# A fused transformer layer on one core: the last four experts' down projection by experts and by quarters, and the output in six transfers

## The reference, cut to what matters

```python
def rms_norm(x, g):
    y = x * lax.rsqrt(jnp.mean(x * x, axis=-1, keepdims=True) + 1e-6)
    return y * g

# h: (256, 2048). One layer: attention and a gated MLP branch, then a mixture of 32 experts
h = h + merged @ w_out
xn2 = rms_norm(h, norm_ffn_g)
# top-1 of 4 groups, top-2 of 8 experts in it; for each of the 32 experts e (FF = 256):
hid = silu(xn2 @ w_e_gate[e]) * (xn2 @ w_e_up[e])          # (tokens, 256)
h = h + combine[:, e] * (hid @ w_e_down[e])                # (tokens, 2048)
return rms_norm(h, norm_final_g)
```

## Time and profile before

| | us |
|---|---|
| runs (3) | 1019.73, 1020.6, 1021.96; median 1020.6 |
| the profiled execution's own time | 1020.6 |
| its span, first to last instruction | 1018.9 |
| around the span | 1.7 |
| mean granted TensorE clock over the span | 0.975 |

### The profile page before, as it was taken

One profiled execution on the slowest core, in us unless ns is written; L12 is line 12 of the kernel. 1 busy time (PEld: TensorE's weight loads), 2 busy tenths in 40 slices (PEclk: granted clock), 3 DMA queues, 4 the chain that ended last, 5 costly groups with the idle time before them and its releaser, 6 DMA issues.

```text
span 1018.9 us, 12972 instructions
## 1 busy us (share of the span) xinstructions
PE 960.7 (94%) x5174; PEld 676.3 (66%) x5174; DVE 392.4 (39%) x535; ACT 331.8 (33%) x482; POOL 2.7 (0%) x13
## 2 busy tenths in 40 slices
PE   8999999999999999999999889999999796979984
PEld 7888788788888888888888555737373541726331
DVE  5746666575555455565443212020202020120204
ACT  5435554744343333443444121121111110211123
POOL 1000000000000000000000000000000000000000
PEclk9999999999999999999999999999999897999978
DMA  9755555559656556666878999999999999999995
GB/s 322 257 196 196 161 159 189 170 176 292 204 197 210 194 193 218 217 246 215 292 285 292 413 421 391 424 420 421 421 421 420 421 421 422 420 421 421 421 400 194
DMA packets 93233, 310.15 MB, mean 304 GB/s; under 512 B 11464, under 2 KB 12544, under 8 KB 71424
## 3 DMA queue, kind: packets, MB, share of 16 engines
q1 hardware_dynamic: 93184, 309.45, 80.1%
HBM read 307.33 MB, written 2.10 MB: 304 GB/s over the span
## 4 chain that ended last, share of the span: by engine, by line
PE 70%; SPq 12%; DMA 12%; ACT 2%; issue 1%; DVE 1%; DVEq 0%; ACTq 0%
PE bank L1381 15%; PE bank L1383 15%; PE bank L1382 15%; SPq L448 12%; DMA pair<-in_w_e_up 10%; PE bank L1689 5%; PE bank L1747 5%; PE bank L1794 2%; PE bank L1708 2%; DMA pair<-in_w_e_down 1%; PE bank L1671 1%; PE bank L1697 1%; PE bank L1451 1%; PE bank L1459 1%; PE bank L1388 1%
## 5 line engine op out<-in xcount | busy, mean ns | idle before, releaser
L893 DVE TENSOR_TENSOR wlo<-raw,whi 128x2048 fp32r<-128x2048 f32 x91 | 208.4, 2291 | 194.6 <-ACT whi L545 194.6
L545 ACT ACTIVATE whi<-raw 128x2048 fp32r<-128x2048 f32 x91 | 174.4, 1917 | 251.0 <-PE bank L1383 246.6
L1381 PE MATMUL bank<-whi,actT_hi 128*128 128x512 f32 x576 | 227.0, 394 | 0.6 <-DVE wlo L893 0.5
L1383 PE MATMUL bank<-wlo,actT_hi 128*128 128x512 f32 x576 | 224.4, 390 | 0.0
L1382 PE MATMUL bank<-whi,actT_lo 128*128 128x512 f32 x576 | 224.2, 389 | 0.0
L1689 PE MATMUL bank<-pair,xe 128*32 128x512 f32 x896 | 118.4, 663 | 22.7 <-DMA pair<-in_w_e_up 22.6
L1381 PEld LDWEIGHTS bank<-whi,actT_hi 128*128 128x128 f32 x576 | 108.2, 188 | 24.0 <-DVE wlo L893 1.2
L1383 PEld LDWEIGHTS bank<-wlo,actT_hi 128*128 128x128 f32 x576 | 108.1, 188 | 22.8
L1382 PEld LDWEIGHTS bank<-whi,actT_lo 128*128 128x128 f32 x576 | 108.2, 188 | 21.6
L1747 PEld LDWEIGHTS bank<-sel,resid 128*128 128x128 f32 x480 | 105.9, 311 | 9.0 <-issue 7.8
L1747 PE MATMUL bank<-sel,resid 128*128 128x128 f32 x480 | 108.6, 384 | 1.0 <-DVE sel L1226 1.0
(11 more groups left out here) (215 smaller groups left out, 724.8 us busy)
## 6 DMA issues: line engine op xcount, KB each, us to landing
pair<-in_w_e_down SPq DMA_DIRECT2D x64, 1024.0 KB, 26.1
pair<-in_w_e_gate SPq DMA_DIRECT2D x56, 1024.0 KB, 26.5
pair<-in_w_e_up SPq DMA_DIRECT2D x56, 1024.0 KB, 26.1
raw<-in_w_gate SPq DMA_DIRECT2D x64, 512.0 KB, 4.5
raw<-in_w_in SPq DMA_DIRECT2D x56, 512.0 KB, 4.8
raw<-in_w_out SPq DMA_DIRECT2D x32, 512.0 KB, 4.8
raw<-in_w_branch_a SPq DMA_DIRECT2D x16, 512.0 KB, 4.5
raw<-in_w_branch_b SPq DMA_DIRECT2D x16, 512.0 KB, 4.6
```

The lines of the kernel that those rows point to most:

```text
L545: return act.activation(whi[slot][:], src, ACT.Copy)
L893: dve.tensor_tensor(wlo[s][:], raw[:, k, :], whi[s][:], ALU.subtract).then_inc(lo_made, 1)
L1381: pe.matmul(o, x_hi, w_hi, start=start, stop=False)
L1383: return pe.matmul(o, x_hi, w_lo, start=False, stop=stop)
```

## The change

Only the last quad and what follows it.

- **Weights.** The first four down pieces of the last quad are those of the other quads: one expert, half f=0, all columns, 8 KB rows. The last four are one block, half f=1, all four experts, 2 KB rows.
- **TensorE.** It waits for all four f=0 pieces, then computes f=0 of blocks 0, 1, 2 and of the first 256 columns of block 3. Then for b = 0, 1, 2: f=1 of block b and at once the scatter of block b; behind that of block 0, f=0 of the second 256 columns of block 3, in bank 2, which is free by then. Then f=1 of both halves of block 3, and the scatter in four quarters of 256 columns, banks 6, 7, 0, 1.
- **Evictions of block 3.** ScalarE takes the first half, VectorE the second.
- **Squares.** Block 3 has four quarters: three on ScalarE, the last on VectorE by a `scalar_tensor_tensor` with an accumulator. `ssq_f` gets a fifth column.
- **The mean.** The step L904 goes: ScalarE takes the root with scale 1/D and a bias tile `eps`, which GpSimd fills at the start of the kernel, and VectorE takes the reciprocal behind it.
- **Output.** `times_gain` is made for blocks 0 and 1 alone. ScalarE multiplies these by the reciprocal root, block by block; VectorE computes blocks 2 and 3 from `resid`, root and gain in one instruction each. Six transfers: four of 256 KB for tile 0, two of 512 KB for tile 1.

The diff, without the branch for tokens over capacity:

```diff
         def down_at(qd, f, e):
-            return PIECES * qd + 4 * QUAD + (2 * e + f if qd == LAST else QUAD * f + e)
+            return PIECES * qd + 4 * QUAD + QUAD * f + e
...
-            return ((6, 7, 0, 1, 2, 3, 4, 5)[u] if qd == LAST else 6 + t), b, t
+            return ((6, 7, 0, 1, 3, 4)[u] if qd == LAST else 6 + t), b, t
+        def last_quarter(i):
+            h, t = divmod(i, TT)
+            return (6, 7, 0, 1)[i], slice(HALF * h, HALF * h + HALF), t
...
+            for h in range(2):
+                sp.wait_ge(y_by_act, h + 1)
+                leave(0, h * COLS, h * COLS + COLS)
+                sp.wait_ge(y_by_dve, h + 1)
+                leave(0, D // 2 + h * COLS, D // 2 + h * COLS + COLS)
+            sp.wait_ge(y_by_act, 4)
+            leave(1, 0, D // 2)
+            sp.wait_ge(y_by_dve, 4)
+            leave(1, D // 2, D)
...
             output_rows_out(LAST, 0)
-            for b in range(1, NC):
-                final_squares(b - 1, sq_f_made, range(0, 1))
-                output_rows_out(LAST, b)
-                final_squares(b - 1, sq_f_made, range(1, 2))
-            final_squares(NC - 1, sq_f_made)
+            for b in range(1, NC - 1):
+                output_rows_out(LAST, b)
+                for t in range(TT):
+                    final_squares(b - 1, t, sq_f_made)
+            final_squares(NC - 2, 0, sq_f_made)
+            act.wait_ge(d_full, NC * LAST + NC)
+            act.activation(out_rows[NC - 1][:, 0:HALF], bank[5][:, 0:HALF], ACT.Copy).then_inc(rows_made, 1)
+            final_squares(NC - 2, 1, sq_f_made)
+            for i in range(3):
+                last_squares(i, sq_f_made)
...
-            root(3)
+            act.wait_ge(ssq_made, 4 * TT)
+            act.activation(ms[:, 3 * TT:4 * TT], ssq[:, 3 * TT:4 * TT], ACT.Sqrt, scale=1.0 / D,
+                           bias=eps[:, 0:1]).then_inc(ms_made, TT)
+            act.wait_ge(rstd_made, 4 * TT)
+            act.wait_ge(hf_early, TT * 2)
             for t in range(TT):
                 n = 3 * TT + t
-                act.activation(y_out[:, t, ACT_COLS], y_out[:, t, ACT_COLS], ACT.Copy,
-                               scale=rstd[:, n:n + 1]).then_inc(y_by_act, 1)
+                for b in range(2):
+                    cols = slice(b * COLS, (b + 1) * COLS)
+                    act.activation(y_out[:, t, cols], y_out[:, t, cols], ACT.Copy,
+                                   scale=rstd[:, n:n + 1]).then_inc(y_by_act, 1)
...
+            dve.wait_ge(d_full, NC * LAST + NC + 1)
+            dve.tensor_copy(out_rows[NC - 1][:, HALF:COLS], bank[2][:, HALF:COLS]).then_inc(rows_late, 1)
+            for i in range(4):
+                dst, cols, t = last_quarter(i)
+                dve.wait_ge(scat_full, 8 * LAST + TT * (NC - 1) + i + 1)
+                h = resid[:, t, (NC - 1) * COLS + cols.start:(NC - 1) * COLS + cols.stop]
+                dve.tensor_tensor(h, bank[dst][:, cols], h, ALU.add).then_inc(added, 1)
+            dve.wait_ge(added, 8 * NQ + 2)
+            order.link(dve.scalar_tensor_tensor(out=sq2[:, 1, D - HALF:D], in0=resid[:, 1, D - HALF:D], scalar=1.0,
+                                                in1=resid[:, 1, D - HALF:D], op0=ALU.mult, op1=ALU.mult,
+                                                accum_out=ssq_f[:, 1, NC:NC + 1]))
...
             dve.tensor_reduce(ssq[:, 3 * TT:4 * TT], ssq_f[:], AX_X, ALU.add).then_inc(ssq_made, TT)
-            inverse_mean(3, D)
...
+            dve.wait_ge(ms_made, 4 * TT)
+            dve.reciprocal(rstd[:, 3 * TT:4 * TT], ms[:, 3 * TT:4 * TT]).then_inc(rstd_made, TT)
...
+                for b in range(2, NC):
+                    cols = slice(b * COLS, (b + 1) * COLS)
+                    dve.scalar_tensor_tensor(out=y_out[:, t, cols], in0=resid[:, t, cols], scalar=rstd[:, n:n + 1],
+                                             in1=gfin[:, cols], op0=ALU.mult, op1=ALU.mult).then_inc(y_by_dve, 1)
...
+            for e in range(QUAD):
+                n = down_at(LAST, 0, e)
+                pe.wait_ge(slot_in[n % RING], arrived(n))
             for b in range(NC):
-                for f in range(2):
-                    n = down_at(LAST, f, b)
-                    pe.wait_ge(slot_in[n % RING], arrived(n))
-                    if f == 0:
-                        pe.wait_ge(rows_made, NC * (LAST - 1) + b + 1)
-                    down_block(LAST, f, b)
-                    if f == 0 and b:
-                        scatter(LAST, range(TT * b - TT, TT * b))
-            scatter(LAST, range(TT * NC - TT, TT * NC))
+                pe.wait_ge(rows_made, NC * (LAST - 1) + b + 1)
+                last_down(0, 2 + b, b, whole if b < NC - 1 else first_half)
+            for b in range(NC - 1):
+                n = down_at(LAST, 1, b)
+                pe.wait_ge(slot_in[n % RING], arrived(n))
+                last_down(1, 2 + b, b, whole)
+                scatter(LAST, range(TT * b, TT * b + TT))
+                if b == 0:
+                    last_down(0, 2, NC - 1, second_half)
+            n = down_at(LAST, 1, NC - 1)
+            pe.wait_ge(slot_in[n % RING], arrived(n))
+            last_down(1, 5, NC - 1, first_half)
+            last_down(1, 2, NC - 1, second_half)
+            for i in range(4):
+                dst, cols, t = last_quarter(i)
+                pe.wait_ge(added, 8 * LAST + i + 1)
...
+                pe.matmul(bank[dst][:, cols], selT[:, t * P:(t + 1) * P], out_rows[NC - 1][:, cols],
+                          start=True, stop=True).then_inc(scat_full, 1)
```

More of the change, by code:

```diff
@@ L190, in build_trunk @@
         table_junk = small("table_junk", [P, 1])
+        eps = small("eps", [P, 1])
         bsT = small("bsT", [P, SG])
@@ L528, in _ @@
             pool.memset(wspT[:], 0.0).then_inc(pool_order, 1)
-            order.n = 6
+            pool.memset(eps[:], EPS).then_inc(pool_order, 1)
+            order.n = 7
             order.wait()
@@ new lines, in _ @@
+            whole, first_half, second_half = slice(0, COLS), slice(0, HALF), slice(HALF, COLS)
+            for e in range(QUAD):
+                n = down_at(LAST, 0, e)
+                pe.wait_ge(slot_in[n % RING], arrived(n))
+            for b in range(NC):
+                pe.wait_ge(rows_made, NC * (LAST - 1) + b + 1)
+                last_down(0, 2 + b, b, whole if b < NC - 1 else first_half)
+            for b in range(NC - 1):
+                n = down_at(LAST, 1, b)
[4 more added lines that the diff above has]
+                    last_down(0, 2, NC - 1, second_half)
@@ new lines, in _ @@
+            n = down_at(LAST, 1, NC - 1)
+            pe.wait_ge(slot_in[n % RING], arrived(n))
+            last_down(1, 5, NC - 1, first_half)
+            last_down(1, 2, NC - 1, second_half)
+            for i in range(4):
+                dst, cols, t = last_quarter(i)
+                pe.wait_ge(added, 8 * LAST + i + 1)
+                if i < TT:
+                    pe.wait_ge(rows_made, NC * LAST + NC)
+                else:
+                    pe.wait_ge(rows_late, 1)
+                pe.matmul(bank[dst][:, cols], selT[:, t * P:(t + 1) * P], out_rows[NC - 1][:, cols],
+                          start=True, stop=True).then_inc(scat_full, 1)
```

92 lines of the change are left out of this document (46 added, 46 removed).

## The result

| | us |
|---|---|
| changed kernel, median of 7 runs | 1024.88 (1023.45 to 1027.99) |
| kernel before, beside it | 1020.21 (1019.61 to 1021.96) |
| ratio | 1.0046, 95% interval 1.0035 to 1.0056 |
| profiled execution | 1027.99, span 1026.2 |

The change costs 4.7 us, in the direction of the forecast and nearly twice its size.

The account below looks back on a forecast made before the run. The prediction took the weights' stream as the bound before and TensorE after the change. Last add 2.86 us later, less 0.40 us in the tail, gave +2.5 on 1020.6: 1023.1, stated as 1023.0, range 1021.8 to 1024.2 (8 in 10: 1020.4 to 1024.7).

Parts of the forecast that it names:

- What bounds: At the end, the weights' stream decides today when the last block starts; after the change TensorE ends last, by 4.6 us.
- The weights' stream: Last quad's down pieces: 8 KB rows save 0.87 us, last landing about 1003.66; f=0 waits for the fourth piece at 991.85.
- rival (c): Last quad's weights: rows of 8 KB bring nothing, fourth piece lands at 992.7, total 1023.9 us; chance 0.10.
- The clock: TensorE in f=0, behind 4.65 us idle: one 3.4 us stretch at half clock, costing 1.7 us.
- Rival (b): TensorE: f=0 and the first f=1 both at half clock, 1.7 us more, total 1024.7 us; chance 0.10.
- Block 3 in halves: Last block, f=1 start to end of last add: 3.66 us instead of 4.52, 0.86 us gained.
- The mean: From last add to first output issue: 2.32 us, 0.53 us sooner than before.
- The output: From first output issue to end of span: 6.95 us plus about 0.13 for 2 KB rows.
- step of 3.7 us: Start of block 3's f=1 on TensorE moves from 1004.57 to 1008.3, 3.7 us later.
- (a): TensorE's clock stays up through f=0, 1.7 us less, total 1021.4 us; chance 0.15.
- (d): Start of the last block: the stream still decides it, gain 2.1 us, total 1018.5 us; chance 0.08.
- (e): Last quad and tail: scatter order doesn't matter, loss in front is won back in the tail, 1020.6 us; chance 0.07.

Follow-up runs that it names:

- after again: The changed kernel run and profiled once more with no edit: 1024.63 us, ratio 1.0028.
- `front_only`: Kernel before with only the new f=0 pieces, wait for all four and order of down blocks; old tail: 1025.17 us, ratio 1.0032.
- `tail_only`: Changed kernel with the down pieces and block order of before, keeping the split last block, new mean and six transfers: 1019.70 us, ratio 0.9980.
- `clock_kept_3`: Changed kernel plus three matmuls of unused result while TensorE waits for the fourth f=0 piece: 1023.51 us, ratio 1.0032.
- `hole_filled`: Changed kernel with each scatter behind the next block's f=1, and ScalarE's block 3 eviction ahead of block 2's squares: 1022.42 us, ratio 1.0022.
- `tail_branch`: `tail_only` with VectorE's square moved behind the branch for tokens over capacity: 1019.75 us, ratio 0.9989; again 1019.91 us, ratio 0.9992.
- `before_again`: The kernel before, unedited, against itself: 1020.67 us beside 1020.70, ratio 1.0002.
- `f0_by_columns`: Changed kernel with the four f=0 pieces as column blocks of all experts (2 KB rows), each used on landing: 1026.18 us, ratio 1.0049.

## Why the forecast was right in direction and short in size

The steps, from the mark on, in us:

| step | forecast | after | after again |
|---|---|---|---|
| last gate/up landing to fourth down piece | 10.05 | 10.02 | 9.97 |
| to the start of f=0 | 0 | 0.24 | 0.24 |
| to the start of block 3's f=1 | 16.45 | 17.31 | 16.81 |
| to the end of the last add | 3.66 | 3.66 | 3.66 |
| to the first output issue | 2.32 | 2.79 | 2.79 |
| to the end of the span | 7.08 | 7.11 | 7.07 |
| sum | 39.56 | 41.13 | 40.54 |

- **What bounds**: right. The stream's hold on the end was lost to TensorE, the last piece lay ready 7.0 and 6.5 us before its use, and `front_only` and `tail_only` put the loss in the half where the forecast had it.
- **The weights' stream**: right to 0.1 us for the fourth piece (the forecast's 10.05 is 0.09 more than its own four times 2.49). 8 KB rows landed every 2.5 us, so it came when forecast, and rival (c) is out. The Trainium skill's line-rate rule (DMA: Bandwidth & Descriptors, Specifications) doesn't hold between 2 and 8 KB here (386 and 425 GB/s). The last piece came 20.5 us behind the mark in both executions, not 21.9, since the forecast counted from a late last landing of the kernel before. The gain was real and worth nothing, as the last piece isn't on the path any more.
- **The clock: this step of the sum failed, the term that was mis-sized most.** I took one low stretch of 3.4 us of work from a single row, 1.7 us of cost. In the first profile the work behind the gap was at half clock for 5.4 us, and the x40 of f=0 and the first f=1 took 6.66 and 6.15 us against 4.07 at full clock: 2.6 and 2.1 us. What that is above the 1.7 (0.9 and 0.4 us) is all by which the start of block 3's f=1 came late (17.31 and 16.81 us for 16.45). Rival (b) had the right mechanism with 3.4 us as its end. The Trainium skill (TensorE: Matmul & The Clock Gate, Why this matters for your kernels) warns of idle gaps between bursts of matmuls. The gaps of 5.94 and 4.50 us agree with that: they cost more than the row behind 0.57 us had shown. But 0.50 was granted without such a gap too (`clock_kept_3`, with TensorE busy for 4.28 of 5 us), which the warning doesn't cover.
- **The start behind the landing.** 0.24 us passed from the fourth piece's landing to the start of f=0, in `front_only` and `hole_filled` too, where before it was 0.04 behind one wait. I had counted none. Four waits stand in a row there, but the first three pieces had landed 2.5 us and more before; what the 0.24 us are isn't shown.
- **Block 3 in halves**: right to the hundredth, 3.66 us. The 128x256 adds took 0.42 us, as the row said.
- **The mean: the second mis-sized term**, 2.79 for 2.32 us. The square was shorter than assumed (0.42, and 0.08 for the accumulator). What I put at nothing is the branch: `order.link` puts a wait for the square's own end right behind the square, ahead of the branch, so that 0.56 us of branching came onto the path. Before, no such wait stood there, the last square was ScalarE's, and 0.1 us passed between it and the reduce. `tail_branch` shows it: 2.33 us with the branch out of the way.
- **The output**: right, 7.1 us. (The text's 5.2 us for 2.1 MB is 5.5 at the 381 GB/s of the earlier trace rows; the sum doesn't use it.)
- **The base.** The sum was made against one execution in which the last block had waited 0.91 us for its piece. In `before_again` that start was 1.1 us earlier relative to the mark. That makes the step of 3.7 us (1004.57 to 1008.3) too short by up to 1.1 us. The premise that the stream decides when the last block starts held in one of the two executions; in the other it decided one step earlier (1.26 us in front of block 3's f=0). What of it holds for the median can't be said from two profiles.

Clock, start and branch together make 1.0 us in one execution and 1.6 in the other; with up to 1.1 for the base, the 2.5 forecast become 3.5 to 5.2, beside the 3.2 and 4.7 measured in two sets. The two sets themselves differ by 1.5 us, nearly all of it in the kernel before (1020.21 and 1021.43), whose runs range from 1019.4 to 1024.2 in the second.

The rivals: (a) and (c) are out, (b) held in part. (d) is out for this kernel, where TensorE came last by 6.5 us and more. (e) is out: the order does matter (`hole_filled`), and the tail wins back 1 us and not all.

## What to carry to other kernels

When weights arrive in a stream that bounds the kernel, look at what the first result needs: a cut that needs four pieces for it turned 4.5 to 5.9 us of the stream's time into idle time here, and the 0.9 us from longer rows didn't pay for that. That cutting the pieces so that each can be used when it lands is by itself the cure wasn't shown (`f0_by_columns`). Leave independent work between an eviction and the matmul that reads what it evicted: each hole was about 0.8 us, and filling them brought some 3 us back. Before moving an instruction onto the last path of a kernel, look at what stands between it and its reader in the engine's program, branches too.

## What the runs showed of the hardware

- The granted clock was at 0.50 for stretches from 3.4 to about 24 us (972 to 996 us, `clock_kept_3`) in these kernels, with TensorE idle and with TensorE busy (4.28 of 5 us there). It differs from run to run in the same place: the same gate/up in front of the gap was granted 1.00 in the first profile of the changed kernel and 0.50 in `clock_kept_3`. Whether the spread of 2 to 4 us between executions of one kernel comes from it isn't shown.
- Idle matmuls meant to hold the clock take nearly twice as long when it is already low: 5.13 us for three of 128x512 (six records) at 0.50, where a scatter of two (four records) takes 1.96 us at 1.00.
- Pieces of 1 MB went at 425 GB/s with 8 KB rows and at 386 with 2 KB rows.
- A `scalar_tensor_tensor` of 128x512 from two float32 tiles in SBUF takes 0.74 us (L1416), a plain two-operand form of the same size 0.68 (L1356).
- A branch that isn't taken cost VectorE 0.56 us where nothing covered it (`after`); out of the way, it gave back 0.46 us on the path (`tail_branch`).
